# Sending one expert body's output rows through DRAM and holding six experts' gate and up weights, in a one-core decoder layer

## The reference, cut to what matters

```python
top_v, top_i = lax.top_k(e_logits, EXPERT_TOP_K)          # 2 of the 8 experts of one group
top_p = jax.nn.softmax(top_v, axis=-1) * g_w
...
hg = jax.nn.silu(einsum('nd,edf->nef', xn, w_gate[g])) * einsum('nd,edf->nef', xn, w_up[g])
y = y + einsum('nef,efd->nd', hg * combine[:, g, :, None], w_down[g])
return h + y
```

## Time and profile before

| | us |
|---|---|
| median of 3 runs | 649.19 |
| the profiled execution | 648.51 |
| its span, first to last instruction | 646.7 |
| TensorE busy in it | 633.2 |
| VectorE, ScalarE, GpSimd busy | 398.7, 203.8, 111.2 |

### The profile page before, as it was taken

The page is one execution under the profiler, slowest core; times in us unless marked ns, Lnnn a source line. Parts: engine busy times, 40 slices in busy tenths (PEclk is TensorE's granted clock), DMA queues, the critical chain, the costliest instruction groups (busy, mean ns, idle before and its releaser), DMA issues.

```text
span 646.7 us, 9803 instructions
## 1 busy us (share of the span) xinstructions
PE 633.2 (98%) x3815; PEld 459.1 (71%) x3815; DVE 398.7 (62%) x739; ACT 203.8 (32%) x417; POOL 111.2 (17%) x168
## 2 busy tenths in 40 slices
PE   5999999999999999999999999999999999999898
PEld 4779999988787878788899995445545453636255
DVE  4747434778997979796855567635354453636145
ACT  6446122234444444424335474200101010101102
POOL 2300025999400000000000010202020202020001
DMA  8542223202232212117154069999999999999933
GB/s 255 152 130 68 66 66 123 74 2 66 66 96 75 76 56 96 51 45 241 66 193 167 33 268 368 420 417 418 420 415 419 418 421 417 419 417 420 406 145 131
DMA packets 45842, 139.04 MB, mean 215 GB/s; under 512 B 6218, under 2 KB 28251, under 8 KB 33508
## 3 DMA queue, kind: packets, MB, share of 16 engines
q1 hardware_dynamic: 43346, 134.70, 54.2%
q0 software_dynamic: 2304, 3.64, 1.5%
q10 hardware_dynamic: 146, 0.07, 0.0%
HBM read 138.95 MB, written 4.19 MB: 221 GB/s over the span
## 4 chain that ended last, share of the span: by engine, by line
PE 91%; DMA 7%; ACT 0%; DVE 0%; issue 0%; SPq 0%; ACTq 0%; DVEq 0%
PE bank L1038 15%; PE bank L656 15%; PE bank L657 14%; PE bank L658 14%; PE bank L1052 7%; DMA w_pair<-in_expert_w_up 6%; PE bank L1130 6%; PE bank L1032 2%; PE bank L898 1%; PE bank L1063 1%; PE bank L1000 1%; PE bank L931 1%; PE bank L966 1%; PE bank L738 1%; PE bank L863 1%; PE bank L930 1%
## 5 line engine op out<-in xcount | busy, mean ns | idle before, releaser
L1038 PE MATMUL bank<-w_pair,xgT 128*64 128x512 f32 x416 | 112.3, 594 | 1.9 <-DMA w_pair<-in_expert_w_up 1.5
L1038 PEld LDWEIGHTS bank<-w_pair,xgT 128*64 128x64 f32 x416 | 36.5, 137 | 57.2 <-issue 57.1
L656 PE MATMUL bank<-whi,xhi 128*128 128x256 f32 x224 | 64.4, 288 | 0.0
L658 PE MATMUL bank<-whi,xlo 128*128 128x256 f32 x224 | 63.0, 281 | 0.0
L657 PE MATMUL bank<-wlo,xhi 128*128 128x256 f32 x224 | 62.9, 281 | 0.0
L656 PE MATMUL bank<-xhi,whi 128*128 128x512 f32 x152 | 62.3, 410 | 0.0
L1669 DVE TENSOR_TENSOR wlo<-wraw,whi 128x2048 fp32r<-128x2048 f32 (+1 forms) x23 | 51.9, 2257 | 16.8 <-ACT whi L1362 16.8
L657 PE MATMUL bank<-xlo,whi 128*128 128x512 f32 x152 | 60.1, 395 | 0.0
L658 PE MATMUL bank<-xhi,wlo 128*128 128x512 f32 x152 | 59.8, 393 | 0.0
L1052 PE MATMUL bank<-w_pair,hT 128*64 128x512 f32 x256 | 56.6, 593 | 1.0 <-DMA w_pair<-in_expert_w_down 1.0
L1582 ACT ACTIVATE hs<-bank 128x256 f32<-128x256 f32 x16 | 6.1, 383 | 156.7 <-PE bank L1038 156.7
(11 more groups left out here) (335 smaller groups left out, 1352.5 us busy)
## 6 DMA issues: line engine op xcount, KB each, us to landing
w_pair<-in_expert_w_down SPq DMA_DIRECT2D x32, 1024.0 KB, 19.3
w_pair<-in_expert_w_gate SPq DMA_DIRECT2D x26, 1024.0 KB, 15.2
w_pair<-in_expert_w_up SPq DMA_DIRECT2D x26, 1024.0 KB, 18.0
wraw<-in_w_in SPq DMA_DIRECT2D x17, 1024.0 KB, 5.5
w_fifth<-in_expert_w_gate SPq DMA_DIRECT2D x6, 1024.0 KB, 16.1
w_fifth<-in_expert_w_up SPq DMA_DIRECT2D x6, 1024.0 KB, 19.0
h<-in_x SPq DMA_DIRECT2D x4, 512.0 KB, 5.3
wraw<-in_w_gla_branch SPq DMA_DIRECT2D x2, 1024.0 KB, 5.3
```

The source lines that it names most:

```text
L656: nc.tensor.matmul(ps, lhi(k), rhi(k), start=(k == 0), stop=False)
L658: last = nc.tensor.matmul(ps, llo(k), rhi(k), start=False, stop=(k == kt - 1))
L1038: last = nc.tensor.matmul(tiles[GU_BANK[s]][j * SLOT:(j + 1) * SLOT, :].rearrange("p (f n) -> p f n", f=2), xgT[:, k, s * P + j * SLOT:s * ...
```

## The change

For the sixth body (i = 5, `ROW_BODY`) the down rows are no longer multiplied with one-hot matrices. ScalarE copies them out of PSUM, and GpSimd writes them by indirect DMA to a DRAM tensor `y_hbm` of 1024 rows, one row for each token and choice. Later eight indirect DMAs read them back by token (four token blocks by two choices), and VectorE adds each to `h` under a mask that tells whether the token has a row of that choice in this body (`member`). The numbers for both ways come from the router's flags: a running count of a token's chosen experts gives the choice. `y_hbm` is filled with zeros early, by eight stores of 512 KB from SyncE behind weight chunk 6. The gate and up weights get a sixth place (`w_sixth`), some buffers move to make room, expert 3 is loaded before expert 2 with the first loads, expert 5 directly behind expert 4, and down loads no longer stand between the two experts of a `next_gate_up`. Semaphores are merged to stay within their number.

```diff
-RING = 5
+RING = 6
+ZERO_AT = 6
+ROW_BODIES = (BODIES - 3,)
@@ routing, weigh(b), for each of four token blocks
+                link(nc.vector.tensor_tensor_scan(flags[:, b, :], ones[:, 0:NE].bitcast(F32), chosen[:, b, :].bitcast(F32), 0.0,
+                                                  ALU.mult, ALU.add))
+                link(nc.vector.tensor_scalar(info[:, b, :, 8:10], flags[:, b, :].rearrange("p (r j) -> p r j", j=2), 1.5, None,
+                                             ALU.is_gt))
@@ VectorE behind weigh(NB - 1), before the loop
+            link(nc.vector.tensor_tensor(which[:, :, :], flags[:, :, e], chosen[:, :, e].bitcast(F32), ALU.mult))
+            for c in range(2):
+                link(nc.vector.tensor_scalar(is_which[:, :, :], which[:, :, :], c + 1.0, None, ALU.is_equal))
+                link(nc.vector.tensor_reduce(in_body[:, c, :], is_which[:, :, :], AX.X, ALU.max))
+                link(nc.vector.scalar_tensor_tensor(back_name[:, c, :], in_body[:, c, :], -4.0 * T, tok[:, 0:NB], ALU.mult, ALU.add))
+                link(nc.vector.tensor_scalar(back_name[:, c, :], back_name[:, c, :], tok[:, NB:NB + 1], (14.0 + c) * T, ALU.add, ALU.add))
@@ TensorE
-                    if i >= 1:
+                    if i >= 1 and i - 1 not in ROW_BODIES:
                         scatter(i - 1, n - 1)
@@ SyncE
+                if c == ZERO_AT:
+                    sp.wait_ge(s_reset, 3)
+                    for q in range(2 * NB):
+                        sp.dma_start(y_hbm[q * P:(q + 1) * P, :], zeros[:, :]).then_inc(s_const, 16)
-                next_gate_up(3, n, (1,))
+                next_down(1, n)
+                next_gate_up(3, n)
                 for i in range(2, BODIES - 2):
                     next_gate_up(2 * i, n)
-                    next_gate_up(2 * i + 1, n, (2 * i - 2, 2 * i - 1))
+                    next_down(2 * i - 2, n)
+                    next_down(2 * i - 1, n)
+                    next_gate_up(2 * i + 1, n)
                 next_gate_up(PAIRS - 4, n)
-                next_down(PAIRS - 6, n)
-                next_down(PAIRS - 5, n)
-                next_gate_up(PAIRS - 3, n)
-                next_down(PAIRS - 4, n)
-                next_down(PAIRS - 3, n)
+                for pair in range(PAIRS - 6, PAIRS - 2):
+                    next_down(pair, n)
             sp.wait_ge(s_mlo, KT)
-            for e in range(2):
+            for e in (0, 1, 3):
                 load_gate(e)
...
             load_up(4)
+            load_gate(5)
@@ VectorE in the last body, ahead of silu and hg of side 1
+                            dve.wait_ge(s_ysc, (r + 1) * (32 * len(ROW_BODIES)))
                             low_rows(n - 1)
+                            rows_added(i - 1)
+                            add_back(0)
@@ and behind add_rows(6)
+                    if i + 1 == BODIES:
+                        rows_added(i)
+                        add_back(1)
+                def add_back(part):
+                    for q in range(4 * part, 4 * part + 4):
+                        b, c = q // 2, q % 2
+                        if q % NB == 0:
+                            dve.wait_ge(s_back[part], (r + 1) * (16 * NB))
+                        dve.wait_ge(s_backadd, r * (2 * NB) + q + 1)
+                        nc.vector.scalar_tensor_tensor(h[:, b, :], back[q % STAGES][:, :], member[:, c, b:b + 1], h[:, b, :],
+                                                       ALU.mult, ALU.add).then_inc(s_backadd, 1)
@@ GpSimd
+                def scatter_rows(i):
+                    for s in range(2):
+                        pool.wait_ge(s_pw, r * BODIES + i + 1)
+                        pool.wait_ge(s_yhi[s], r * (2 * BODIES) + 2 * i + 2)
...
+                        nc.gpsimd.indirect_dma_start(out=y_hbm, out_offset=bass.IndirectOffsetOnAxis(ap=y_no[:, 2 * i + s:2 * i + s + 1], axis=0),
+                                                     in_=y_rows[ROW_BODIES.index(i)][s][:, :], in_offset=None, ...).then_inc(s_ysc, 16)
+                def rows_back():
+                    pool.wait_ge(s_ysc, (r + 1) * (32 * len(ROW_BODIES)))
+                    pool.wait_ge(s_gu[1], (r + 1) * BODIES - 1)
...
+                    for q in range(2 * NB):
...
+                        nc.gpsimd.indirect_dma_start(out=back[k][:, :], out_offset=None, in_=y_hbm,
+                                                     in_offset=bass.IndirectOffsetOnAxis(ap=back_no[:, q % 2, q // 2:q // 2 + 1], axis=0), ...)
```

More of the change, by code:

```diff
@@ L426, in layer_kernel @@
         onehotT = [[more(f"onehotT{i}{j}", [P, NB, P], F32R) for j in range(2)] for i in range(2)]
-        hs = [more(f"hs{i}", [P, FF]) for i in range(2)]
         hg = [more(f"hg{i}", [P, FF]) for i in range(2)]
+        hs = hg
         hT = [more(f"hT{i}", [P, 2, P]) for i in range(2)]
+        y_rows = [[at(f"y_rows{k}{s}", place[0] + (2 * k + s) * 4 * K1, [P, D]) for s in range(2)] for k in range(2)]
         y_hi = [more(f"y_hi{i}", [P, D], F32R) for i in range(2)]
         y_lo = [more(f"y_lo{i}", [P, D], F32R) for i in range(2)]
-        assert place[0] <= 80 * K1, place[0] / K1
+        y_hbm = nc.dram_tensor("y_hbm", (2 * T, D), F32, kind="Internal").ap()
+        assert place[0] <= 64 * K1, place[0] / K1
         w_pair = [at(f"w_pair{s}", WE + 6 * s * 8 * K1, [P, 2, 3, KT * FF]) for s in range(2)]
@@ L542, in layer_kernel @@
         s_wd = sem2("down_loaded")
+        s_ysc = sem("rows_scattered")
+        s_back = [sem(f"rows_back{k}") for k in range(2)]
+        s_backadd = sem("rows_back_added")
         s_sc = [sem(f"scatter_bank{i}_full") for i in range(4)]
@@ L629, in slots, with direct @@
             c = 32 * (j % 2) + 16 * s
-            return tiles[W_BANK][:, c:c + 8]
+            return tiles[W_BANK][:, c:c + 10]
         def ring_loads(n, e):
             return 32 * (n * len(range(e % RING, NE, RING)) + e // RING + 1)
+        def direct(r, i):
+            return r * ADDED + sum(1 for k in range(i) if k not in ROW_BODIES)
         def scatter_bank(i, u):
@@ L1242, in next_gate_up @@
                     load_gate(e)
-                    for done in between:
-                        next_down(done, n)
-                    between = ()
             def next_down(pair, n):
@@ L1279, in _ @@
             sp.wait_ge(*banks.emptied(("unit", WO + 1, NB - 1)))
-            for e in range(2, 4):
-                load_gate(e)
+            load_gate(2)
+            load_down(1, (1,))
+            sp.wait_ge(s_sq2, 4 * NB)
             load_down(1, (0,))
-            sp.wait_ge(s_sq2, 4 * NB)
-            load_down(1, (1,))
             sp.wait_ge(*banks.filled(("logits", NB - 1)))
@@ L1598, in _ @@
         def _(dve):
-            link = chain(dve, s_dve)
+            linked = [0]
+            link = chain(dve, s_dve, linked)
             norms = [0]
@@ L1983, in slot_weights @@
                         else:
-                            link(nc.vector.tensor_scalar(row_name[:, s:s + 1], slots(0, s)[:, 0:1], slots(0, s)[:, 1:2], None, ALU.add))
+                            link_in_round(nc.vector.tensor_scalar(row_name[:, s:s + 1], slots(0, s)[:, 0:1], slots(0, s)[:, 1:2], None, ALU.add))
                         dve.wait_ge(s_idx[s], r * BODIES + j + 1)
+                        if j in ROW_BODIES:
+                            p = 2 * j + s
+                            for half in range(2):
+                                rows = slice(half * SLOT, (half + 1) * SLOT)
+                                placed = nc.vector.scalar_tensor_tensor(y_name[rows, p:p + 1], slots(j, s)[rows, 8 + half:9 + half],
+                                                                        float(T), row_name[rows, p:p + 1], ALU.mult, ALU.add)
+                                link_in_round(placed)
+                            link_in_round(nc.vector.tensor_scalar(y_no[:, p:p + 1], y_name[:, p:p + 1], 2.0 * T, None, ALU.add))
                         for half in range(2):
@@ L2022, in low_rows, with rows_added, add_rows @@
                         last.then_inc(s_ylo[s], 1)
-                def add_rows(i, n):
+                def rows_added(i):
+                    for k in range(4):
+                        dve.wait_ge(s_add[k], 2 * direct(r, i) + 1)
+                def add_rows(i):
                     for u in range(8):
@@ L2054, in _ @@
                         low_rows(n, (0,))
-                    elif 2 <= i < BODIES - 1:
+                    elif 2 <= i < BODIES - 1 and i - 1 not in ROW_BODIES:
                         low_rows(n - 1)
@@ L2060, in _ @@
                         low_rows(n, (1,))
-                    if i >= 1:
-                        add_rows(i - 1, n - 1)
+                    if i >= 1 and i - 1 not in ROW_BODIES:
+                        add_rows(i - 1)
+                    if i + 1 == BODIES:
+                        rows_added(i)
+                        add_back(1)
+                    elif i == ROW_BODY - 1:
+                        rows_back_known()
```

(5 more changed lines are left out.)

172 lines of the change are left out of this document (115 added, 57 removed).

## The result

The changed kernel takes 650.97 us, median of 7 runs (650.05 to 653.66); the kernel before, timed beside it, 649.25 us (7 runs, 648.94 to 650.11). The ratio is 1.0028 with a 95% interval of 1.0019 to 1.0038: slower, by little more than the least that can be told. The forecast was 650.6. The profiled execution took 650.05 us, 1.54 more than the one of before.

A forecast was written before the change was run, and what follows sets the result against it. The prediction took DMA and TensorE as both full, the last weights' landing setting the date; -4.4 (earlier loads) + 3.4 (order) + 1.8 (traffic) + 0.6 (tail) = +1.4 on 649.2 gave 650.6 us, range 646.6 to 653.0 for 8 in 10.

The forecast's parts named there:

- What bounds the kernel: Bodies: DMA engines and TensorE both full; last needed load's landing sets the date, some 8 us of TensorE work becomes waiting.
- 1, the scatter: Body 6: 32 scatter matmuls, 7.33 us, leave TensorE; by itself this gives nothing, only an earlier wait for loads.
- TensorE is the bound: Rival: TensorE's work sets the time, so waits and scatter go, stall and tail come: -6.3, 642.9 us; chance 7%.
- 2, loads earlier: Expert 3 moves into the idle DMA stretch at 356 to 372; all later loads 4.4 us earlier, bounds 3.5 to 5.0.
- 3, the order: Last body: a down matrix lands last instead of expert 31, so half a down side follows: +3.4 us, or 0.
- the order costs nothing: Rival: last down half lands together with expert 31, or the end wait is met otherwise: -2.0, 647.2 us; chance 15%.
- 4, the rows' traffic: Row writes 1.3 us and 0.5 of the reads' 1.4 precede the last weights: +1.8 us, bounds 1.3 and 2.9.
- 5, routing: Body 1, near 401: 13 added VectorE instructions delay the one-hots; TensorE stalls 2.7 us, hidden by its wait for loads.
- 6, the adds: Last body on VectorE: first four adds just fit before hg; four more delay the tail +0.6 us, bounds 0 and 1.
- 7, zeros: Eight zero stores between 56 and 70, some 10 us of DMA, stay hidden; chunk 7 otherwise some 3 us late.
- The late reads: Rival: in the last body the fourth read lands later than 617.1, holding up hg and the scatter: 651.9 us; chance 18%.
- The sum: Whole kernel: -4.4 + 3.4 + 1.8 + 0.6 = +1.4 us, last load landing at 610.2, median 650.6 us; chance 60%.

The follow-up runs named there:

- Experiment 7: Changed kernel with 4 MiB less to load (only 64 gate and up columns of experts 30 and 31): 655.26 us, ratio 1.0080 to the kernel before.
- experiment 3: Changed kernel without its row way: sixth body's scatter back on TensorE, six places and new load order kept: 647.93 us, ratio 0.9971 to the kernel before.
- experiment 4: Kernel before with expert 3 loaded among the first loads, five places, expert 31 last: 646.38 us, ratio 0.9956 to the kernel before.
- experiment 12: Changed kernel without its row way (scatter on TensorE, six places), expert 31 loaded last: 645.51 us, ratio 0.9944 to the kernel before.
- experiment 11: Changed kernel, expert 31 last, last two pairs' down loads issued after four reads land, 4 MiB less to load: 646.23 us, ratio 0.9953.
- 8: Kernel before with 4 MiB less to load (only 64 gate and up columns of experts 30 and 31): 646.11 us, ratio 0.9953 to the kernel before.
- experiment 1: Changed kernel with expert 31 loaded behind the down loads of pairs 12 and 13, as before: 654.95 us, ratio 1.0077 to the kernel before.
- experiment 6: Changed kernel with both row scatters and all eight reads issued but moving next to nothing: 650.06 us, ratio 1.0012 to the kernel before.

## Why the prediction was right, point by point

- **What bounds the kernel.** Right: the last load of the down weights set the date (609.67, said 610.2), and the 7.3 us of the scatter turned into waiting: 2.6 us at 401, and in the last body 6.65 where 2.34 stood before. There about 8 were said; 1.4 of them went into the slower matmuls at 604.36. Experiment 7 shows it directly (with 4 MiB less to load the 6.3 us wait is gone), and experiments 3, 4 and 12 from the other side: they only change the loads, and the kernel gets faster. One step of the reading was loose. The list of what stood in the queue at 588 is 10 MiB with expert 31 itself, which is 25.1 us and fits the 24.69; the text has 8 MiB. Nothing in the sum rests on it.
- **1, the scatter.** Right. What it is worth where loads are not late was over-estimated. The rival "TensorE is the bound" had the change at 6.3 us, 2.3 of them the waits that the kernel before also loses there. Of the other 4.0, 3.8 are there in experiment 11 against 8 until the scatter of body 6 starts. They are lost behind it, 2.1 by the late `y_lo` and 1.7 by the lower clock that follows. In 7 against 8 the late reads make it a loss of 9.2.
- **2, loads earlier.** Expert 4's up weights landed at 401.8, said 401.2: -3.8 in place of -4.4, inside its bounds.
- **3, the order.** Right in its size (3.4; 3.6 in experiment 1, 3.0 in experiment 12). The rival built on it, "the order costs nothing, 647.2", was wrong as a forecast of this kernel: taking the 3.4 us away brings 654.95, as the late reads take their place.
- **4, the rows' traffic.** Over-sized: 1.8 said, with 1.3 as the lower bound. The medians of experiment 6 give 0.9. In the profiles the time from the landing of expert 4's up weights to the last landing was 207.9 us in the changed kernel, and without this traffic 207.2 in the kernel before, 207.0 in experiment 3 and 206.2 in experiment 6. That is 0.7 to 1.7; single executions can't settle it closer.
- **5, routing.** 2.6 us of stall, said 2.7, and hidden. What I missed is what follows it in other executions (below).
- **6, the adds.** Mis-sized: the last scatter starts 16.5 us behind the first, 15.2 before: +1.3, said +0.6, above its bound of 1. The four adds take 5.2 us, not 4.9, and the first begins 0.3 us after the last add of `h`, which the sum had at nothing.
- **7, zeros.** Hidden, as said: ScalarE takes chunk 7 at 75.86 after the same 11.09 us of waiting for TensorE.
- **The late reads.** Here the fourth read landed at 610.2, 6.9 us ahead of the date from which it decides. I had both its issue (603.8, not 608.2 at the latest) and its landing (6.4 us, not 9.7) at the slow end. But the reason that I gave against it, a quarter of the rows, was not the one: in experiment 1 a read of a quarter takes 12.5 us. In the changed kernel TensorE's own wait for down weights keeps SyncE from refilling the down places until 609.5, and so keeps the queues clear for the reads. That wait is what I counted as pure loss.
- **The sum.** Against the kernel before: earlier loads -3.8 (said -4.4), traffic +0.7 (+1.8), order +3.4 (+3.4), tail +1.3 (+0.6). That is +1.6, against the 1.54 measured and the 1.4 said. The mechanism was right, but three of the four terms are off by 0.6 to 1.1 us, on both sides; that the total fits to 0.2 is luck.

## What to carry to other kernels

When two resources are full, find the date that both wait for, and change the order of transfers before moving work: one load moved into an idle stretch gave 0.44% here (experiment 4), and 0.56% with six places and the old order at the end (experiment 12), where the change with all its new machinery lost 0.28%. The new order at the end was itself a loss of some 2 to 3 us. If a transfer becomes something that an in-order engine waits for, ask which loads the engine's own progress sets free at that moment, and hold them back if they have time. A wait can protect another: before it is removed, look at what is issued when it ends.

## What the hardware did that was not expected

**The granted clock after a short wait.** In the changed kernel TensorE waits 6.3 us for down weights, and the 16 matmuls behind it take 5.10 us in place of 3.65 (the row at 604.36 against the one at 609.81). It cost nothing, as the next weights came at 609.67. In experiments 1 and 7 the same cost some 2.3 us on the path. The 2.6 us stall at 401 did it too, but not in every execution. Of the nine profiles with this stall eight have a granted clock of 0.50 to 0.75 from 404 to 408, and the changed kernel's has 1.00. In experiment 1 the 32 matmuls behind the stall took 8.62 us (7.0 elsewhere):

```profile
404.43 8.62 PE L1063 MATMUL bank<-w_pair,xgT 128*64 128x512 f32 x32
```

Kernels that have this stall scatter over 1.6 to 7.8 us between runs, experiment 1 most: its one run with a mean granted clock of 1.000 took 649.42, the others, at 0.988 to 0.995, took 653.6 to 657.2. Experiments 3, 4 and 12, without the stall and with a mean clock of 1.000, stay within 1.0 to 1.7. The kernels with the stall also have longer waits in the last body, so that these runs don't say how much of the scatter is the stall's. The Trainium skill, TensorE: Matmul & The Clock Gate, in its section on the clock gate, says that the array's clock falls to half after TensorE has been idle, and that waits for weights in a matmul stream bring this about. The trace agrees: behind the 7.71 us wait of experiment 7 the clock was 0.50. That a stall of 2.6 us does it in some executions and not in others is the runs' alone.

**Indirect DMAs beside loads.** They pass a queue of 20 us, as the prediction said: in the changed kernel the two writes landed after 8.0 us (median), while a down load issued at 589.03 took 20.64. The Trainium skill, DMA: Bandwidth & Descriptors, section Queues, rings and completion order, says that an engine takes turns between the queue rows, and these landings agree with it. But passing isn't free. A read landed after 2.9 us on quiet engines, 6.4 beside the end of a queue, and 12.5 with four loads issued in its midst. I had used one figure, that of the gathers, for all.
